# Splitting heads 1 and 2's normed tokens where they lie, and moving two products of head 2 ahead of its projections

## The chip, the cores and the metric

The kernel runs on one core of one Trainium2 chip. The metric is the device time of one launch, in microseconds (us); a lower time is better. The engines are named as in the profile: PE is TensorE (matmuls), PEld its weight loads, DVE is VectorE, ACT is ScalarE, POOL is GpSimd and SP is SyncE, which here only issues DMAs.

## The reference, cut to what matters

Two layers of an encoder step run on 576 tokens (512 of a prompt, 64 of a sample), 1024 features wide. In each layer the tokens are normed and go through one wide projection, whose columns feed a short convolution, a latent attention with eight heads, and two gates:

```python
h = rmsnorm(x, g_pre_mix)
z = h @ w_in
b_g, c_g, xin, cq, ckv_raw, kpe_raw, ga, gb = jnp.split(z, ...)
yc, new_buf = short_conv(c_g * xin, conv_buf, conv_w)
y_a = b_g * yc
q = (rmsnorm(cq, g_q) @ w_uq).reshape(B, L, N_HEADS, QK_DIM)
y_b = mla_attention(q_nope, q_pe, pos, ckv_all, kpe_all, k_pos, w_uk, w_uv)
merged = jax.nn.sigmoid(ga) * y_a + jax.nn.sigmoid(gb) * y_b
x = x + rmsnorm(merged @ w_o, g_post_mix)
x = x + rmsnorm(jnp.square(jax.nn.relu(rmsnorm(x, g_pre_ffn) @ w1)) @ w2, g_post_ffn)
```

## The kernel before, in words

**Precision.** Every fp32 product is made of three matmuls. Each operand is split into a high part (an ACT copy into a rounded format) and a low part (a DVE subtraction, original minus high part), and `mm3` (L809 to L813) adds low weight times high token, high weight times low token and high times high. So each weight block and each token tile passes through one ACT instruction and then one DVE instruction before PE can use it.

**Layout.** Features lie on the 128 partitions, in eight rows of tiles (k = 0 to 7); the 576 tokens lie along the free axis, in two halves of 288. The high and low parts of the tokens are `xs_hi` and `xs_lo` (`pl.xh`, `pl.xl`). A projection of 128 columns for one half is 24 matmuls of 288 columns ("a block half").

**Plain and mixed heads.** Per layer eight heads run one after the other. Heads 0, 1 and 7 are plain: five weight blocks, each for two halves, on tokens that are only scaled by the gain, with the norm factor applied afterwards. Heads 2 to 6 are mixed: two pairs of blocks (c = 0 and 1) are each computed by seven products of half size (12 matmuls each) instead of eight, in Winograd's manner, and two more half-blocks (`mixed_block`) make the fifth. These products need the truly normed tokens, and four tiles of differences of them, called turned: `turn_raw` is made by `head_mix(t)` on DVE, and split into `turn_hi` (ACT) and `turn_lo` (DVE, `head_mix_lo`). Products 0, 1 and 6 use normed tokens, products 2, 3, 4 and 5 use turned tiles 1, 2, 3 and 0 (`TURN_ORDER`).

**Where the normed tokens lie before.** During heads 0 and 1 DVE norms the tokens in place, in `x` (`normed_rows`, semaphore `h_made`). The four `turn_hi` tiles occupy just the memory of `x`, so before they are written SP stores the normed tokens to DRAM (`h_store`, three DMAs of 864, 864 and 576 KB, L961 to L963, at positions 0, 1 and 2 of head 1). When head 1's last block (block 4) has read the old `xs_hi`, SP loads them back into the memory of `xs_lo` (`h_load`, four DMAs of 576 KB, L956 to L959, in the order `H_ORDER`). ACT copies each quarter into `xs_hi` (`normed_hi`, L1590 to L1594) and DVE subtracts in place (`normed_head_lo`, L2484 to L2488).

**Order.** There is no planner: each engine's order is written out by hand, and semaphores join them. PE's order in head 1 is block 0, projections, block 1, scores, block 2, turns (transposes of the probabilities), block 3, attended (probabilities times values), block 4. In a mixed head it is products 0 to 3, projections, products 4 to 6, scores, `mixed_block`, turns, products 0 to 2 of the second pair, attended, products 3 to 6. Head 2 alone begins with its projections, before products 0 to 6. The projections of an even head are: rotary query for two halves (9 matmuls each), keys (6 matmuls of 512), values in two parts (12 matmuls of 256 each), query for two halves (9 each). They wait within for DVE: keys for `pv_read` (DVE has read the old attention result, in `attention_out`), values part 1 and the first query half for the two rotary sums, the second query half for `keys_lo`.

**Ring.** The products go through four PSUM banks in turn. A product may start when the bank that was filled four products earlier has been emptied: product 0 by the ACT copy `snapshot`, product 1 by `upper_left`, 2 by `first_difference`, 3 by `second_sum` and so on, on DVE.

**Other queues.** SP issues all weight loads, the loads of the small attention weights of the next head (`even_small`, five DMAs, L865 to L873) in position 2 of head 1, and the store of each finished head's row. POOL issues, in layer 0 only, DMAs that add up weight blocks for both layers' mixed heads (`weight_sums`); they share the DMA engines with SP's loads. In head 1 ACT splits the small weights (L1228) before it copies the transposed probabilities (L1494), so attended hangs on the small weights' arrival.

Of the kernel before, what the change touches and what calls it, by code (L numbers as in the profile page):

```python
# [15 lines left out]
P = 128  # L16
# [162 lines left out]
H_ORDER = ((0, 0), (4, 0), (4, 1), (0, 1))  # L179
# [176 lines left out]
class Plan:  # L356


    def __init__(self, nc, ctx):
# [4 lines left out]
        self.h_kept = nc.dram_tensor("h_kept", (P, KC, NT), F32, kind="Internal").ap()  # L364
# [138 lines left out]
        self.h_stored = semaphore("h_stored")  # L503
        self.h_landed = [semaphore("h_landed0"), semaphore("h_landed1"), semaphore("h_landed2"), semaphore("h_landed3")]
# [294 lines left out]
def cols(s):  # L799
    return slice(NH * s, NH * (s + 1))  # L800
# [52 lines left out]
def loads(nc, block, pl, x_in, consts, tables, blocks, small, uv, cache_t, cache_n, cache_pe, x_out):  # L853
# [3 lines left out]
    def _(sp):  # L857
# [39 lines left out]
        for L in range(DEPTH):  # L897
# [58 lines left out]
            def h_load(n):  # L956
                k0, half = H_ORDER[n]
                sp.dma_start(pl.xlraw[:, k0:k0 + 4, cols(half)], pl.h_kept[:, k0:k0 + 4, cols(half)]) \
                    .then_inc(pl.h_landed[n], 16)  # L959

            def h_store(n):  # L961
                rows = slice(3 * n, min(3 * n + 3, KC))
                sp.dma_start(pl.h_kept[:, rows, :], pl.x[:, rows, :]).then_inc(pl.h_stored, 16)  # L963

# [18 lines left out]
            for h in range(HEADS):  # L983
# [3 lines left out]
                if h == 1:  # L987
                    sp.wait_ge(pl.h_made, KC * (L + 1))
                if h == HEADS - 1:
                    sp.wait_ge(pl.my_stored, stored(L, HEADS - 2))  # L990
                for j in range(HEAD_POS[h + 1] - HEAD_POS[h]):
# [8 lines left out]
                    if (h, j) == (FIRST_MIXED - 1, 4):  # L1000
                        sp.wait_ge(pl.ring_full, full(L, r_hd(h, 4, 0)))
                        sp.wait_ge(pl.h_stored, 48 * (L + 1))
                        h_load(0)
                        h_load(1)
                        sp.wait_ge(pl.ring_full, full(L, r_hd(h, 4, 1)))
                        h_load(2)
                        h_load(3)
                    elif is_mixed(h):
# [6 lines left out]
                    if h == FIRST_MIXED - 1 and j < 3:  # L1015
                        h_store(j)
# [185 lines left out]
def scalar_engine(nc, block, pl, x_in, x_out, kv_out, kpe_out, conv_out):  # L1202
# [4 lines left out]
    def _(eng):  # L1207
# [121 lines left out]
        for L in range(DEPTH):  # L1329
# [172 lines left out]
            def plain_head(h):  # L1502
# [2479 lines left out]
```

## Time and profile before

| | us |
|---|---|
| median of 3 runs | 1723.73 (1723.25 to 1723.8) |
| the profiled execution, its own time | 1726.3 |
| its span (first to last instruction) | 1724.5 |
| PE busy | 1705.7 (99%) |
| DVE busy | 1309.3 (76%) |
| ACT busy | 855.1 (50%) |

The granted clock of TensorE was 0.997 of full speed over the span. The profile splits the span into slices and names, for each idle time of an engine, what ended it; "L811" is a line of the program, which for matmuls is a line of the helper `mm3`. In the timelines a row gives the start, the duration, the engine, the line, the operation with output and inputs, and a count of merged instructions; square brackets hold the idle time before it and what ended that. Matmuls overlap, so that the step from one start to the next (0.13 us for 288 columns) is what one costs. Head 1's attended part to head 2's turns lies at 134 to 177 us in layer 0 and at 989 to 1028 us in layer 1.

### The profile page before, as it was taken

The page shows a single profiled execution, that of the slowest core. Times are in us where ns is not written, and L with a number is a line of the kernel's source. Part 1 is how long each engine was busy: PE and PEld are TensorE (multiplying, and loading weights), DVE is VectorE, ACT ScalarE, POOL GpSimd, SP SyncE. Part 2 cuts the span into 40 slices and gives each one's busy share as a digit, 9 for nine tenths or more (in the row PEclk, how much of TensorE's full clock was granted, in tenths as well). Part 3 has the DMA queues.
Part 4 walks back from the last instruction along what each step waited for, and adds up shares of the span by engine and source line. Part 5 has one row for each costly group of instructions (what it writes and reads, how often), then busy time and mean ns, then how long its engine had stood idle before and what let it go on. Part 6 is the DMA issues. An engine that isn't in the chain of part 4 may idle for free.

```text
span 1724.5 us, 31894 instructions
## 1 busy us (share of the span) xinstructions
PE 1705.7 (99%) x12735; PEld 1690.9 (98%) x12735; DVE 1309.3 (76%) x2514; ACT 855.1 (50%) x1665; POOL 122.3 (7%) x163
## 2 busy tenths in 40 slices
PE   9999999999999999999999999999999999999997
PEld 9998999999999999999999999999999999999997
DVE  7788787767798786668687797777678887777665
ACT  7625454545465454436366364545435536444452
POOL 1412121212210000000001000000000000000000
PEclk9999999999999999999999999999999999999998
DMA  7899898898762232323124454343532213322231
GB/s 239 198 212 244 214 209 211 178 249 235 163 129 97 89 96 86 99 86 111 60 84 149 148 166 139 114 121 112 171 117 98 99 37 111 98 86 87 74 99 55
DMA packets 90996, 231.54 MB, mean 134 GB/s; under 512 B 9824, under 2 KB 25440, under 8 KB 90848
## 3 DMA queue, kind: packets, MB, share of 16 engines
q1 hardware_dynamic: 71968, 185.45, 33.5%
q0 software_dynamic: 17600, 41.95, 13.8%
q8 instruction: 101, 1.65, 0.4%
q10 hardware_dynamic: 1280, 2.10, 0.3%
q14 instruction: 47, 0.39, 0.1%
HBM read 214.39 MB, written 57.02 MB: 157 GB/s over the span
## 4 chain that ended last, share of the span: by engine, by line
PE 94%; DMA 2%; DVE 2%; ACT 1%; SPq 1%; issue 0%; DVEq 0%; ACTq 0%
PE ring L811 19%; PE ring L813 19%; PE ring L812 19%; PE att L811 11%; PE att L813 11%; PE att L812 11%; PE att L3527 1%; DMA cache_pe_raw<-cache_pe_in 1%; PE att L806 1%; PE att L805 1%; DMA small_raw<-small_in 1%; DMA xs_lo_raw<-h_kept 1%; PE att L818 0%; ACT rope_s L1291 0%; PE att L3343 0%
## 5 line engine op out<-in xcount | busy, mean ns | idle before, releaser
L811 PE MATMUL ring<-xs_hi,w_lo 128*128 128x288 f32 x1872 | 556.6, 297 | 4.3 <-DVE xs_lo L2744 2.2
L813 PE MATMUL ring<-xs_hi,w_hi 128*128 128x288 f32 x1872 | 551.4, 295 | 0.0
L812 PE MATMUL ring<-xs_lo,w_hi 128*128 128x288 f32 x1872 | 551.3, 294 | 0.0
L2071 DVE TENSOR_TENSOR w_lo<-w_raw,w_hi 128x1024 fp32r<-128x1024 f32 (+1 forms) x364 | 370.0, 1035 | 37.3 <-ACT w_hi L1220 27.2
L811 PEld LDWEIGHTS ring<-xs_hi,w_lo 128*128 128x128 f32 x1872 | 351.6, 188 | 7.3 <-DVE ga L2355 2.4
L812 PEld LDWEIGHTS ring<-xs_lo,w_hi 128*128 128x128 f32 x1872 | 351.7, 188 | 1.4
L813 PEld LDWEIGHTS ring<-xs_hi,w_hi 128*128 128x128 f32 x1872 | 351.5, 188 | 0.0
L813 PE MATMUL att<-f_hi,w_hi 128*128 128x288 f32 x960 | 283.2, 295 | 0.0
L812 PE MATMUL att<-f_lo,w_hi 128*128 128x288 f32 x960 | 282.9, 295 | 0.0
L811 PE MATMUL att<-f_hi,w_lo 128*128 128x288 f32 x960 | 282.6, 294 | 0.0
L811 PEld LDWEIGHTS att<-f_hi,w_lo 128*128 128x128 f32 x960 | 180.4, 188 | 0.0
L812 PEld LDWEIGHTS att<-f_lo,w_hi 128*128 128x128 f32 x960 | 180.4, 188 | 0.0
L813 PEld LDWEIGHTS att<-f_hi,w_hi 128*128 128x128 f32 x960 | 180.4, 188 | 0.0
L1212 ACT ACTIVATE w_hi<-w_raw 128x1024 fp32r<-128x1024 f32 x98 | 101.9, 1053 | 87.0 <-DMA w_raw<-blocks_in 86.8
L1220 ACT ACTIVATE w_hi<-w_raw 128x1024 fp32r<-128x1024 f32 x118 | 122.8, 1051 | 7.2 <-DMA w_raw<-blocks_in 6.5
L2923 DVE TENSOR_TENSOR my<-att,my 128x288 f32<-128x288 f32 x160 | 70.8, 451 | 67.7 <-PE att L813 67.7
L813 PE MATMUL ring<-mix_hi,w_hi 128*128 128x288 f32 x384 | 113.5, 295 | 0.0
L811 PE MATMUL ring<-mix_hi,w_lo 128*128 128x288 f32 x384 | 113.1, 295 | 0.0
L812 PE MATMUL ring<-mix_lo,w_hi 128*128 128x288 f32 x360 | 105.9, 294 | 0.0
L811 PE MATMUL ring<-turn_hi,w_lo 128*128 128x288 f32 x320 | 94.9, 296 | 0.0
L812 PE MATMUL ring<-turn_lo,w_hi 128*128 128x288 f32 x320 | 94.4, 295 | 0.0
L813 PE MATMUL ring<-turn_hi,w_hi 128*128 128x288 f32 x320 | 94.2, 295 | 0.0
(342 smaller groups left out, 3184.4 us busy)
## 6 DMA issues: line engine op xcount, KB each, us to landing
w_raw<-blocks_in SPq DMA_DIRECT2D x195, 512.0 KB, 3.7
weight_sums<-blocks_in POOLq DMA_DIRECT2D x80, 256.0 KB, 7.2
w_raw<-blocks_in SPq DMA_DIRECT2D x62, 256.0 KB, 4.6
weight_sums<-blocks_in POOLq DMA_DIRECT2D x20, 512.0 KB, 5.6
weight_sums<-weight_sums POOLq DMA_DIRECT2D x40, 256.0 KB, 7.6
w_raw<-weight_sums SPq DMA_DIRECT2D x20, 512.0 KB, 4.6
w_raw<-weight_sums SPq DMA_DIRECT2D x40, 256.0 KB, 4.4
small_raw<-small_in SPq DMA_DIRECT2D x16, 320.0 KB, 4.6
```

The lines of the kernel that those rows point to most:

```text
L805: pe.matmul(out, both, keys[1], start=False, stop=False)
L806: return pe.matmul(out, both, keys[0], start=False, stop=True)
L811: pe.matmul(out, w[1], x[0], start=first, stop=False)
L812: pe.matmul(out, w[0], x[1], start=False, stop=False)
L813: return pe.matmul(out, w[0], x[0], start=False, stop=last)
L1212: act.activation(hi, raw, ACT.Copy).then_inc(pl.weights_hi, 1)
L1220: act.activation(hi, raw, ACT.Copy).then_inc(pl.weights_hi, 1)
L2071: return dve.tensor_tensor(out, a, hi.bitcast(F32), ALU.subtract)
L2923: dve.tensor_tensor(dst, src, dst, ALU.add).then_inc(pl.w2_free, 1)
L3527: last = pe.transpose(att[:, to:to + P], pl.probs[:, PO[t] + P * j:PO[t] + P * (j + 1)], ident)
```

## The change: what it does

The store and the reload are gone, with their semaphores and SP's wait for `h_made` at the start of head 1. ACT splits the normed tokens straight from `x` into `xs_hi` as soon as block 4 of head 1 has read the old half, and DVE subtracts from `x`; the quarters come in a new order (rows 0 to 3 and 4 to 7 of half 0, then of half 1). The turned high parts, which overwrite `x`, now wait for the low parts of the normed tokens and come after them. PE runs products 0 and 1 of head 2 before the head's projections, the rest after. The split of weight position 12 (`at + 2`), which head 1 did last, moves into head 2.

```diff
-H_ORDER = ((0, 0), (4, 0), (4, 1), (0, 1))
+H_ORDER = ((0, 0), (4, 0), (0, 1), (4, 1))
 # SP
-                if h == 1:
-                    sp.wait_ge(pl.h_made, KC * (L + 1))
-                    if (h, j) == (FIRST_MIXED - 1, 4):
-                        sp.wait_ge(pl.ring_full, full(L, r_hd(h, 4, 0)))
-                        sp.wait_ge(pl.h_stored, 48 * (L + 1))
-                        h_load(0)
-                        h_load(1)
-                        sp.wait_ge(pl.ring_full, full(L, r_hd(h, 4, 1)))
-                        h_load(2)
-                        h_load(3)
-                    if h == FIRST_MIXED - 1 and j < 3:
-                        h_store(j)
 # ACT, end of head 1
-                next_weight(3)
-                if h == FIRST_MIXED - 1:
-                    eng.wait_ge(pl.turn_made, 4 * (L + 1))
-                    eng.wait_ge(pl.h_stored, 48 * (L + 1))
-                    for t in TURN_ORDER:
-                        act.activation(pl.th[t][:, :, :], pl.traw[t][:, :, :], ACT.Copy).then_inc(pl.turn_hi, 1)
-                else:
+                if h != FIRST_MIXED - 1:
+                    next_weight(3)
                     next_weight(4)
 # ACT, head 2
                 def normed_hi(n):
-                    eng.wait_ge(pl.h_landed[n], 16 * (L + 1))
-                    act.activation(pl.xh[tile], pl.xlraw[tile], ACT.Copy).then_inc(pl.h_hi, 1)
+                    eng.wait_ge(pl.ring_full, full(L, r_hd(h - 1, 4, half)))
+                    eng.wait_ge(pl.h_made, KC * (L + 1))
+                    act.activation(pl.xh[tile], pl.x[tile], ACT.Copy).then_inc(pl.h_hi, 1)
+                def turned_hi_of(i):
+                    t = TURN_ORDER[i]
+                    eng.wait_ge(pl.turn_made, 4 * (L + 1))
+                    eng.wait_ge(pl.h_lo, 4 * L + (3 if t < 2 else 4))
+                    act.activation(pl.th[t][:, :, :], pl.traw[t][:, :, :], ACT.Copy).then_inc(pl.turn_hi, 1)
                 def even_projections():
...
                     if h == FIRST_MIXED:
-                        normed_hi(0)
+                        turned_hi_of(1)
                     keys_hi(h)
                     rotary_hi(h)
-                    if h == FIRST_MIXED:
-                        normed_hi(1)
                     values_hi(h, 0)
                     values_hi(h, 1)
                     if h == FIRST_MIXED:
-                        normed_hi(2)
+                        turned_hi_of(2)
+                        turned_hi_of(3)
+                        pos_hi(L, at + 2)
                     query_hi(h)
                     rotary_sample(h)
                 if h == FIRST_MIXED:
+                    for n in range(4):
+                        normed_hi(n)
+                    turned_hi_of(0)
+                    snapshot(0)
                     even_projections()
                     pos_hi(L, at + 3)
-                    normed_hi(3)
-                    snapshot(0)
 # DVE, end of head 1
-                next_weight(3)
+                if h != FIRST_MIXED - 1:
+                    next_weight(3)
-                elif h == FIRST_MIXED - 1:
-                    head_mix_lo(0)
-                    head_mix_lo(1)
                 attention_out(h)
+                    normed_head_lo(0)
                     gated_out(h, 0)
+                        normed_head_lo(1)
                     gated_out(h, 1)
+                        normed_head_lo(2)
                     merge(h, slice(0, NP_), pl.merged)
 # DVE, head 2
                     rotary_sum(h, 0)
                     rotary_sum(h, 1)
-                        normed_head_lo(0)
                     keys_lo(h)
+                        head_mix_lo(0)
                     rotary_lo(h)
-                        normed_head_lo(1)
                     values_lo(h, 0)
                     values_lo(h, 1)
-                        head_mix_lo(2)
+                        head_mix_lo(1)
                     query_lo(h, 0)
                     query_lo(h, 1)
                 if h == FIRST_MIXED:
+                    upper_left(0, pl.cv[:, cols(0)])
+                    normed_head_lo(3)
                     even_projections()
+                    pos_lo(L, at + 2)
+                    head_mix_lo(2)
                     head_mix_lo(3)
-                    upper_left(0, pl.cv[:, cols(0)])
-                    pos_lo(L, at + 3)
                     first_difference(0)
-                    normed_head_lo(2)
+                    pos_lo(L, at + 3)
                     second_sum(0)
-                    normed_head_lo(3)
 # PE, mixed head
-                if h == FIRST_MIXED:
-                    projections(h)
-                for i in range(4):
+                ahead = 2 if h == FIRST_MIXED else 4
+                for i in range(ahead):
                     product(h, 0, i)
-                if h != FIRST_MIXED:
-                    projections(h)
-                for i in range(4, 7):
+                projections(h)
+                for i in range(ahead, 7):
                     product(h, 0, i)
```

PE's own waits for `h_lo` follow the new order: one quarter for product 0, two for product 1, four for product 6.

## Rows read from the trace of the kernel before

**Rows 1.** The page's first part: busy time, share of the span, instructions.
```profile
PE 1705.7 (99%) x12735; PEld 1690.9 (98%) x12735; DVE 1309.3 (76%) x2514; ACT 855.1 (50%) x1665; POOL 122.3 (7%) x163
```
**Rows 2.** PE's waits over the span: total us, times, longest.
```profile
PE att L811 <- DVE probs_t_lo L2071: 2.4, 1, 2.4
PE ring L811 <- DVE xs_lo L2744: 2.2, 1, 2.2
...
PE ring L811 <- DVE xs_lo L2071: 0.7, 2, 0.4
```
**Rows 3.** Timeline of PE in layer 0 (start, us, what, idle before).
```profile
133.74 0.29 PE L813 MATMUL ring<-xs_hi,w_hi 128*128 128x288 f32 x1
136.47 0.50 PE L811 MATMUL att<-probs_t_hi,v_lo 128*128 128x512 f32 x1 [2.44 <-DVE probs_t_lo L2071]
...
148.01 0.50 PE L811 MATMUL att<-ckv_hi,small_lo 128*128 128x512 f32 x1 [0.62 <-DVE rx L2454]
...
177.43 1.26 PE L3527 MATMUL att<-consts,probs 128*128 128x128 f32 x10
```
**Rows 4.** Timeline of PE in layer 1, same stretch.
```profile
989.16 0.39 PE L811 MATMUL att<-probs_t_hi,v_lo 128*128 128x512 f32 x1
...
991.01 0.34 PE L811 MATMUL ring<-xs_hi,w_lo 128*128 128x288 f32 x1
...
997.43 0.29 PE L811 MATMUL att<-cqn_hi,small_lo 128*128 128x288 f32 x1
...
1006.78 0.29 PE L811 MATMUL ring<-xs_hi,w_lo 128*128 128x288 f32 x1
...
1018.47 0.22 PE L818 MATMUL att<-q,small_hi 128*128 128x128 f32 x1
...
1028.45 1.25 PE L3527 MATMUL att<-consts,probs 128*128 128x128 f32 x10
```
**Rows 5.** Timeline of ACT in layer 1.
```profile
991.73 4.32 ACT L1576 ACTIVATE turn_hi<-turn_raw 128x1152 fp32r<-128x1152 f32 x4
998.83 3.32 ACT L1291 ACTIVATE rope_s<-att 32x288 f32<-32x288 f32 x8 [2.77 <-PE att L813]
...
1003.86 1.80 ACT L1467 ACTIVATE q_pe<-rope_t 64x288 fp32r<-64x288 f32 x4
...
1009.64 1.08 ACT L1220 ACTIVATE w_hi<-w_raw 128x1024 fp32r<-128x1024 f32 x1
```
**Rows 6.** Timeline of DVE in layer 1.
```profile
994.17 1.22 DVE L2071 TENSOR_TENSOR w_lo<-w_raw,w_hi 128x1024 fp32r<-128x1024 f32 x1
995.31 2.62 DVE L2071 TENSOR_TENSOR turn_lo<-turn_raw,turn_hi 128x1152 fp32r<-128x1152 f32 x2
...
1000.58 0.46 DVE L2386 TENSOR_TENSOR rope_t<-att,cos 128x288 f32<-128x288 f32 x1 [0.43 <-ACT rope_s L1291]
...
1004.75 0.68 DVE L2071 TENSOR_TENSOR k_lo<-att,k_hi 128x512 fp32r<-128x512 f32 x1
1005.46 1.87 DVE L2071 TENSOR_TENSOR q_pe<-rope_t,q_pe 64x288 fp32r<-64x288 f32 x4
...
1008.64 1.28 DVE L2071 TENSOR_TENSOR v_lo<-att,v_hi 128x512 fp32r<-128x512 f32 x2
...
1011.11 0.81 DVE L2071 TENSOR_TENSOR q<-att,q 128x288 fp32r<-128x288 f32 x2
```
**Rows 7.** The chain that ended last, in order of time (start, us, what).
```profile
122.53 10.03 DMA small_raw<-small_in
...
378.11 12.65 DMA cache_pe_raw<-cache_pe_in
```
**Rows 8.** DMA issues from 207 to 222 us (count, KB, us to landing).
```profile
small_raw<-small_in SPq DMA_DIRECT2D x1, 192.0 KB, 6.7
```
**Rows 9.** DMA issues from 290 to 305 us, same columns.
```profile
small_raw<-small_in SPq DMA_DIRECT2D x1, 192.0 KB, 10.6
```
**Rows 10.** Busy us by engine (instructions), granted clock, DMA share, GB/s, 62 to 140.
```profile
62.00:140.00 78.00, 75.10 (x554) 73.66 (x553) 57.74 (x115) 34.00 (x67) 18.32 (x26) 1.00 0.85 203
```

More of the change, by code:

```diff
@@ L954, in pos_load @@
                     sp.dma_start(pl.half_slot(s, k)[2], piece).then_inc(pl.slots[s], 16)
[L956 to L963, printed above, removed]
             def my_load(n):
@@ L999, in _ @@
                         sp.dma_start(pl.naraw[:, :, :], cache_n[L]).then_inc(pl.nat_landed, 16)
[L1000 to L1008 removed]
+                    if is_mixed(h):
                         sp.wait_ge(pl.ring_full, full(L, r_mixed(h, (1, 3, 5, 8, 9, 11, 13, 15)[j])))
@@ L2487, in normed_head_lo @@
                 eng.wait_ge(pl.h_hi, 4 * L + n + 1)
-                minus(pl.xl[tile], pl.xlraw[tile], pl.xh[tile]).then_inc(pl.h_lo, 1)
+                minus(pl.xl[tile], pl.x[tile], pl.xh[tile]).then_inc(pl.h_lo, 1)
             def plain_head(h):
@@ L2580, in plain_head @@
                     own.step(dve.tensor_tensor(pl.ga[:, :], pl.ga[:, :], pl.rx[:, :], ALU.mult))
-                next_weight(3)
+                if h != FIRST_MIXED - 1:
+                    next_weight(3)
                 if h < FIRST_MIXED - 1:
                     next_weight(4)
-                elif h == FIRST_MIXED - 1:
-                    head_mix_lo(0)
-                    head_mix_lo(1)
                 attention_out(h)
                 own.wait()
+                if h == FIRST_MIXED - 1:
+                    normed_head_lo(0)
                 if h < HEADS - 1:
                     gated_out(h, 0)
+                    if h == FIRST_MIXED - 1:
+                        normed_head_lo(1)
                     gated_out(h, 1)
+                    if h == FIRST_MIXED - 1:
+                        normed_head_lo(2)
                     own_ring(h, 4, 1)
@@ L2653, in even_projections @@
                     rotary_sum(h, 1)
+                    keys_lo(h)
                     if h == FIRST_MIXED:
-                        normed_head_lo(0)
-                    keys_lo(h)
+                        head_mix_lo(0)
                     rotary_lo(h)
-                    if h == FIRST_MIXED:
-                        normed_head_lo(1)
                     values_lo(h, 0)
@@ L2669, in mixed_head @@
                 if h == FIRST_MIXED:
+                    upper_left(0, pl.cv[:, cols(0)])
+                    normed_head_lo(3)
                     even_projections()
+                    pos_lo(L, at + 2)
+                    head_mix_lo(2)
                     head_mix_lo(3)
-                    upper_left(0, pl.cv[:, cols(0)])
+                    first_difference(0)
                     pos_lo(L, at + 3)
-                    first_difference(0)
-                    normed_head_lo(2)
                     second_sum(0)
-                    normed_head_lo(3)
                 else:
@@ L3574, in product @@
                     if i in (0, 1, 6):
-                        eng.wait_ge(pl.h_lo, 4 * L + (0, 1, 6).index(i) + 1)
+                        eng.wait_ge(pl.h_lo, 4 * L + (1 if i == 0 else 2 if i == 1 else 4))
                     else:
```

4 lines of the change are left out of this document (removed).

## The prediction

> **What bounds the kernel now.** The first view is the page's busy part: PE is busy 1705.7 of 1724.5 us [rows 1], so a change can only move PE's waits. The second, PE's waits, is short [rows 2]: the ones that this change can touch are 2.4 us for the transposed probabilities and 0.7 us (two waits, one per layer) for the low parts of the normed tokens; 2.2 us lie at the end of layer 0. The third, PE's timeline over head 1's end and head 2, puts numbers to the whole stretch. I measure it from the point at which attended may start to the turns of head 2. In layer 1 attended starts without a wait at 989.16 and the turns at 1028.45: 39.3 us [rows 4]. In layer 0 the block before attended issues its last matmul at 133.74, so attended could start at 133.87; it starts at 136.47, and the turns at 177.43: 43.6 us [rows 3].
>
> **The stretch without any wait.** From rows 4: attended 1.85 (989.16 to 991.01), block 4 6.42 (to 997.43, which is 48 matmuls at 0.133 each). Products of 12 matmuls are 1.59 each, so seven are 11.1. The projections lie between 997.43 and 1006.78: 9.35, of which some 0.25 is waiting for `keys_lo`; 9.1. Scores and `mixed_block` last from 1018.47 to 1028.45: 10.0. Together 38.5. So layer 1 waits 0.8 us in all, layer 0 5.1 us: 2.6 before attended, the rest in four small waits, the first of them before keys [rows 3]. More than 5.9 us is not to be had from this stretch.
>
> **What goes.** The store and the reload move 4.7 MB per layer. Layer 0's 2.6 us comes from the small weights: their last DMA took 10.03 us to land from its issue at 122.53 [rows 7], with two stores of 864 KB issued before it. Attended started 3.9 us after that landing, so a landing before 130.0 would clear it. Without a store in front, the same 192 KB DMA landed in 6.7 us in one later head and in 10.6 us in another [rows 8, 9]; issued at about 122.1 it lands between 128.8 and 132.7. Two ends, then: the wait goes (2.6), or it stays (0). I take the first, as the stores' bytes were ahead of it here, and keep the other as a rival. From 62 to 140 us the DMA engines moved 203 GB/s [rows 10]. On this the Trainium skill (DMA: Bandwidth & Descriptors, section Queues, rings and completion order) says that each DMA engine takes turns between its queue rows, packet by packet. By that rule SP's row had half of 203 GB/s beside POOL's, an estimate, and 864 KB less in front is up to 8.7 us earlier, which clears the wait outright; the 10.6 us of rows 9, with no store ahead, does not fit so simple a picture.
>
> The small waits of both layers (2.5 and 0.8) come from the old order of DVE work and go with it; what matters is what the new order puts there.
>
> **The new order, worked through on layer 1's clock.** Steps: ACT's split of 1152 columns 1.08 from start to start (four end within 4.32), of a weight 0.95; DVE's 1.27 and 1.14; a result is seen by another engine about 0.05 us after the end, by PE 0.13 [rows 5, 6]. DVE reaches the point where `w_lo` started, 994.17, and now goes straight to `attention_out` (0.7, where before 3.7 us of splits came first).
>
> Block 4's first half is full at 994.4. ACT copies quarter 0 until 995.6, DVE subtracts until 997.0; product 0 could start at 997.43: no wait, by 0.3. `gated_out` (0.37), quarter 1 until 998.7; product 1 at 999.02: no wait, by 0.2. `gated_out` of half 1 (0.5), quarter 2 from 999.1 to 1000.4, `merge` to 1001.0. ACT has finished quarters 2 and 3 at 999.9, but the first turned copy waits for quarter 2's low part: 1000.5 to 1001.6, and `snapshot` ends at 1002.0. DVE stands idle 1.1 us for it, then `upper_left` and quarter 3 until 1003.7. PE has begun the projections at 1000.6.
>
> The rotary swaps take ACT 1.66 per half [rows 5]: 1002.0 to 1005.3. The rotary sums (1.2 each: both lie between the start at 1000.58 and 1003.5, one 1.27 split ahead of `k_lo`, with a wait between them) follow at 1003.8 and 1005.4 and end at 1005.1 and 1006.7; PE wants them at 1005.8 and 1007.3. ACT: turned copy, then keys until 1007.0; `keys_lo` [rows 6] until 1007.7, wanted at 1008.5. So the projections run through and product 2 can start at 1009.7. Its low part, the first turned subtraction, ends at 1009.0: in time.
>
> Then DVE has before product 3: four rotary subtractions (1.88), two of the values (1.2), and the second turned subtraction (1.35) [rows 6]: 1008.9 + 1.9 + 1.2 + 1.35 = 1013.4. Product 3 could start at 1011.3; it starts at 1013.5: **a new wait of 2.2**. Product 4 could start at 1015.1, but behind the turned subtraction lie `query_lo` twice (0.75), the moved weight 12 (1.14) and the third turned subtraction (1.35): 1013.3 + 0.75 + 1.14 + 1.35 = 1016.5, so **a second new wait of 1.5**. The fourth ends at 1017.8, product 5 needs it at 1018.3; `first_difference` and weight 13 end by 1019.3, product 6 needs them at 1019.9. Scores start at 1021.5 and the turns at 1031.45, against 1028.45. DVE's later duties (masks, maxima, probabilities) shift with the scores, as their own chain has 1 us more room than before.
>
> The same procedure, run on the old order with the same steps, gives 1028.36 where the trace has 1028.45, so I trust it to a few tenths. The bounds of the two waits: nothing, if DVE were never idle while waiting for ACT (it idles 2.9 us from 994.17 to 1007, and 2.9 earlier leaves 0.8 of the 3.7), and 1.5 us more per layer, if quarters 0 and 1 come late for products 0 and 1, whose margins are 0.3 and 0.2.
>
> **Sum.** Attended to turns becomes 1031.45 - 989.16 = 42.3 us in both layers, since the order is the same and layer 0's DMAs no longer stand in it. Layer 1: 42.3 - 39.3 = +3.0. Layer 0: 42.3 - 43.6 = -1.3. Together +1.7 us on the profiled execution's 1726.3, so 1728.0 (span 1726.2). The median of the runs was 1723.73, 2.6 lower; +1.7 on it is **1725.4**. PE's clock was at its full level (1.00) in a stretch with the 2.44 us wait in it [rows 10], and no new wait is longer, so I charge nothing for it.
>
> **Rivals.**
> *A, the new waits don't come* (the order lets products 3 and 4 through, because DVE and ACT are quicker together than I add up). All 5.9 us go: 1717.8. For it: 5.9 us of waits are really there. Against: DVE was full in this stretch before, and its work now begins with idle time.
> *B, the small weights still land late in layer 0* (the other side). Place: ACT's split before the transposed probabilities. Price: up to 2.6 us, from a landing after 130.0. With it layer 0 is +1.3 and the sum +4.3: 1728.0. For it: rows 9. Against: 1.7 MB less in front of it.
> *C, the wait at the end of layer 0 goes too.* It followed a cache DMA of 12.65 us [rows 7] beside POOL's sums; fewer bytes and another phase may bring it in early: 2.2 less and some 0.3 of restart, +1.7 - 2.5 = -0.8, so 1722.9. The same phase could make it worse by as much, but less likely.
> *D, the removed DMAs were hidden and the order costs nothing either*: no change from 1723.7 within 1 us; layer 0's 2.6 would have to stay and the new waits be half mine.
>
> **How the numbers follow.** Forecast (within 1.3 us of 1725.4) 0.55; A 0.10; B 0.17; C 0.11; D 0.07. The measurement can tell about 0.2%, 3.4 us, from no change, so faster means below 1720.3 and slower above 1727.2. Faster: A and a little of C, 0.12. Slower: B with the forecast's upper edge, 0.22. Same: 0.66. The range leaves out most of A and the far end of B: 1721 to 1728.8; the forecast's own is 1724.1 to 1726.7.
>
> **What would show it.** PE's waits after: the 2.4 us for the probabilities gone in layer 0 (else B); no wait of products 0 and 1 for quarters 0 and 1; a wait of about 2.2 us before product 3 and 1.5 us before product 4 in both layers, ended by DVE's turned subtraction; from attended to turns 42.3 us twice. If that distance is below 40 us I am wrong in the order of DVE's work (A); if products 0 or 1 wait, in head 1's end; and if both distances are right while the time is not, something outside this stretch moved (C).

## The result, and the profile after

The median after is 1732.43 us (7 runs, 1729.27 to 1734.06) where the kernel before had 1723.8 beside it (7 runs, 1723.25 to 1729.72). The ratio of the two is 1.0033, 95% interval 1.0021 to 1.0045. A second comparison gave 1.0034 (1.0022 to 1.0046), with 1730.76 against 1724.59. So the change costs 5.7 to 5.9 us by the ratio; the forecast was +1.7. The time lies outside the range given, 1721 to 1728.8.

The forecast also stood on a narrow base. The kernel before was run some 150 times more beside the experiments: its medians were 1724.6 to 1726.7 and its single times 1720.9 to 1732.1. The three runs shown ahead of the prediction (1723.25 to 1723.8) lay below all of these medians. Ratios are taken within a comparison and don't suffer from it.

The profiled execution after took 1730.14 us, its span is 1728.3: 3.8 more than before. PE's waits of the kernel after (total, times, longest) come first.

```profile
PE ring L808 <- DVE turn_lo L2051: 7.3, 4, 2.4
PE ring L808 <- DVE xs_lo L2727: 2.7, 1, 2.7
```

Against [rows 2] the 2.4 us for the probabilities and the 0.7 us for the low parts of the normed tokens are gone, and four waits for the turned subtraction have come. PE's timeline of the kernel after shows them, with the points that the forecast measured from:

```profile
133.71 0.39 PE L808 MATMUL att<-probs_t_hi,v_lo 128*128 128x512 f32 x1
...
158.28 0.37 PE L808 MATMUL ring<-turn_hi,w_lo 128*128 128x288 f32 x1 [2.35 <-DVE turn_lo L2051]
...
161.42 0.37 PE L808 MATMUL ring<-turn_hi,w_lo 128*128 128x288 f32 x1 [1.31 <-DVE turn_lo L2051]
...
176.25 1.25 PE L3510 MATMUL att<-consts,probs 128*128 128x128 f32 x10
...
989.99 0.39 PE L808 MATMUL att<-probs_t_hi,v_lo 128*128 128x512 f32 x1
...
1014.57 0.37 PE L808 MATMUL ring<-turn_hi,w_lo 128*128 128x288 f32 x1 [2.35 <-DVE turn_lo L2051]
...
1017.70 0.37 PE L808 MATMUL ring<-turn_hi,w_lo 128*128 128x288 f32 x1 [1.31 <-DVE turn_lo L2051]
...
1032.53 1.25 PE L3510 MATMUL att<-consts,probs 128*128 128x128 f32 x10
```

In layer 0 attended starts at 133.71 without a wait and the turns at 176.25: 42.5 us. In layer 1 they start at 989.99 and 1032.53: again 42.5 us, where the forecast said 42.3 twice. DVE's own timeline of layer 1 has the work that the forecast queued ahead of products 3 and 4:

```profile
1008.58 1.35 DVE L2051 TENSOR_TENSOR turn_lo<-turn_raw,turn_hi 128x1152 fp32r<-128x1152 f32 x1
1009.96 1.87 DVE L2051 TENSOR_TENSOR q_pe<-rope_t,q_pe 64x288 fp32r<-64x288 f32 x4
1011.87 1.29 DVE L2051 TENSOR_TENSOR v_lo<-att,v_hi 128x512 fp32r<-128x512 f32 x2
1013.07 1.35 DVE L2051 TENSOR_TENSOR turn_lo<-turn_raw,turn_hi 128x1152 fp32r<-128x1152 f32 x1
1014.34 0.82 DVE L2051 TENSOR_TENSOR q<-att,q 128x288 fp32r<-128x288 f32 x2
1015.07 1.22 DVE L2051 TENSOR_TENSOR w_lo<-w_raw,w_hi 128x1024 fp32r<-128x1024 f32 x1
1016.20 2.62 DVE L2051 TENSOR_TENSOR turn_lo<-turn_raw,turn_hi 128x1152 fp32r<-128x1152 f32 x2
```

So in this pair of executions layer 0's turns come 1.2 us earlier (forecast 1.3), and layer 1's stretch is 3.25 longer (forecast 3.0). Together 2.05 of the 3.8 us. Another 2.0 came between layer 0's turns and layer 1's attended, where nothing was changed: 811.7 us before and 813.7 after. (Behind layer 1's turns the kernel after is 0.2 quicker.) The row that shows it is the first product with wo in layer 0, and the granted clock behind it. PE's timeline after, and then the windows (columns as in [rows 10]):

```profile
402.16 0.45 PE L808 MATMUL ring<-xs_hi,w_lo 128*128 128x288 f32 x1 [2.73 <-DVE xs_lo L2727]
402.41 0.44 PE L809 MATMUL ring<-xs_lo,w_hi 128*128 128x288 f32 x1
```

```profile
400.00:402.00 2.00, 0.00 (x0) 0.00 (x0) 1.97 (x7) 0.92 (x3) 0.00 (x0) 1.00 0.73 154
402.00:404.00 2.00, 1.84 (x8) 1.87 (x9) 2.00 (x7) 0.12 (x1) 0.54 (x1) 0.58 0.97 302
404.00:406.00 2.00, 2.00 (x11) 2.00 (x10) 2.00 (x5) 0.10 (x1) 1.12 (x2) 0.57 0.55 79
406.00:408.00 2.00, 2.00 (x18) 2.00 (x16) 1.48 (x3) 2.00 (x6) 0.00 (x0) 1.00 0.88 124
```

The wait is 0.5 us longer than the 2.2 of [rows 2]. After PE's wait of 2.73 us the clock goes from its full level (2.4 GHz) towards the lower one (1.2 GHz): matmuls follow each other in 0.24 in place of 0.13 us for 14 steps, some 1.5 us. What ended the wait is further back, in the chain and on ACT. First the chain after, then ACT's timeline:

```profile
376.24 13.75 DMA cache_pe_raw<-cache_pe_in
```

```profile
390.02 1.06 ACT L1532 ACTIVATE cache_t_hi<-cache_t_raw 128x1024 fp32r<-128x1024 f32 x1 [3.32 <-DMA cache_pe_raw<-cache_pe_in]
```

The fetch was issued 1.9 us earlier than before but took 13.75 us in place of 12.65 [rows 7]. Part of what PE had gained by then was given back.

A caution on sizes: the second profiled execution of the kernel after has 3.7 us of wait at this place, and a single pair can't give the median's difference. That needs the experiments.

### The profile page after: what moved, and what is told of

Read it like the earlier page. It is cut to its first block, busy times and chain, and to the rows that moved or that the text cites. A ratio compares the mean times of both kernels' runs of the same rounds, so it can differ in the third digit from the quotient of the medians.

```text
span 1728.3 us, 31890 instructions
## 1 busy us (share of the span) xinstructions
PE 1706.8 (99%) x12735; PEld 1692.9 (98%) x12735; DVE 1311.5 (76%) x2514; ACT 854.5 (49%) x1665; POOL 122.4 (7%) x163
## 4 chain that ended last, share of the span: by engine, by line
PE 95%; DVE 2%; ACT 1%; DMA 1%; issue 0%; SPq 0%; DVEq 0%; ACTq 0%
PE ring L808 19%; PE ring L810 19%; PE ring L809 19%; PE att L808 11%; PE att L810 11%; PE att L809 11%; PE att L3510 1%; DMA cache_pe_raw<-cache_pe_in 1%; PE att L803 1%; PE att L802 1%; ACT rope_s L1267 1%; DVE turn_lo L2051 0%; PE att L815 0%; PE ring L3346 0%; PE att L3326 0%
```

## The experiments

Theories that are called by a letter are stated in the expectations.

**Once more, and three first guesses.** *after_again* is the kernel after, for a second profile. *reorder* puts the weight-12 split back into head 1, takes `snapshot` ahead of the first turned copy, the low parts of the first two quarters ahead of `gated_out`, and all turned splits and `first_difference` ahead of the rotary, value and query splits, on ACT and DVE:

```diff
@@ DVE, head 2
-                    even_projections()
-                    pos_lo(L, at + 2)
+                    head_mix_lo(0)
+                    rotary_sum(h, 0)
+                    rotary_sum(h, 1)
+                    keys_lo(h)
+                    head_mix_lo(1)
                     head_mix_lo(2)
                     head_mix_lo(3)
                     first_difference(0)
                     pos_lo(L, at + 3)
+                    rotary_lo(h)
...
```

> The changed kernel, unchanged, to see what differs from run to run. Its profiled execution took 1730.1 us, of which +3.3 lie in layer 1's head 2, -1.3 in layer 0's heads 1 and 2, +0.5 in a longer wait at the end of layer 0 and +1.6 in a stretch of 3.4 us at 402 us where the granted clock was 0.58; yet most other runs took 1732 to 1734 at a lower mean clock. Theory K (clock): a run's time follows its mean granted clock, about 1.7 us more for each 0.001 below 0.997, because TensorE falls to its lower level after one or more of the waits (2.4 and 1.3 in each layer's head 2, 2.7 at the end of layer 0); the new trace has 402 us or the heads' waits followed by matmuls at 0.24 us a step. Theory D (DMA): the runs differ in the wait at the end of layer 0, which hangs on a cache load; the trace then shows that wait outside 2.2 to 2.8 us with the clock unchanged. Median 1732 by both.

> The changed kernel with DVE and ACT in another order in head 2: the split of weight position 12 back in head 1, the second normed quarter's subtraction ahead of the first gated output, and all turned splits ahead of the rotary, value and query splits. By the same step arithmetic that gave the waits of 2.2 and 1.5 us, none is left: turns 38.7 us after attended in both layers (changed kernel: 42.5). Both theories: both waits gone in both layers, 3.7 us each. Theory K: the falls of the clock after them go too, leaving the one after the end of layer 0 in some runs: median 1721 to 1724.5, 8 to 11 below the changed kernel. Theory D: 7.5 below, 1725.

*after_again*: 1.0034; its waits of PE are 7.2 us (4) for `turn_lo` and 3.7 before wo. The clock was lower in 160 to 170 (0.66) and in 400 to 420 us. *reorder*: 1722.24, ratio 0.9981 (0.9968 to 0.9994). No wait before products 3 and 4 is left in either layer, and layer 1's stretch is 38.7 us. So the new waits were a matter of the order of the splits on DVE and ACT, as forecast, and with another order the change can pay (a gain of 0.2%, near what can be told).

*fill_all* puts matmuls that nobody reads into the waits, to see whether the clock then stays up and what that is worth; *fill_heads* does it in head 2 alone. *before_store_late* moves the second of the three stores of normed tokens in the kernel before behind the small weights, where the third already stood.

```diff
+                    if h == FIRST_MIXED and i in (3, 4):
+                        fill(r_mixed(h, i), 17 if i == 3 else 10)
...
+            if L == 0:    # this part in fill_all only
+                fill(WO_A[0], 40, False)
```

> The changed kernel with idle matmuls put where PE waits: 17 of 288 columns before product 3 and 10 before product 4 of head 2 (both layers), 40 of 128 columns before the first output product of layer 0. They write the bank that the next product overwrites and take no longer than the waits. Theory K: the waits are as long as before but PE is active in them, so the clock stays at its upper level: mean clock 0.997 or more in every run and 1727 to 1728.5 us, 4 to 5 us below the changed kernel and with a spread under 1 us. Theory D: the time stays at 1730 to 1734.

> The kernel after with matmuls into an unused place of PSUM in head 2's new waits: 17 of 288 columns before product 3 (about 2.4 us) and 10 before product 4 (about 1.5 us), in both layers; their results are read by nobody. Nothing is changed at the end of layer 0. Theory K: the waits are filled, no clock fall at 160 or 1017 us, and the waits themselves stay; against the kernel after 1 to 2 us less on the median (ratio to before 1.0025). Theory D: no change against the kernel after (ratio 1.0034), and the wait at 402 to 407 us is there with 2 to 4 us.

> The kernel before with one step moved: SP issues the second store of normed tokens (864 KB) behind the small weights of head 2 instead of in front of them. If the stores in front made these land late (step 2 of the prediction), the wait of 2.4 us before attended in layer 0 shrinks to under 0.5 us and the rest stays: profile 1723.7, median 1721.5 against 1723.8. If POOL's sums alone make them late, the wait stays within 0.5 us of 2.4 and the time within 0.7 us.

*fill_all*: 1.0034 (1.0021 to 1.0047) with the clock at full level in every 10-us window up to 1700; its fill before wo took 4.66 us and outlasted the wait by some 0.8, which hides part of what it gave. *fill_heads*: 1.0033 (1.0018 to 1.0048), waits in the heads filled, 4.0 us of wait before wo with a lower clock behind it. Theory K had asked 4 to 5 us of *fill_all*, so the clock is not the main cause. A smaller part of it, the 1 to 2 us that K gave *fill_heads* (ratio 1.0025), lies inside that run's interval and is not excluded. *before_store_late*: 1.0000 (0.9989 to 1.0011). The wait for the probabilities went in its profile, as expected of a store in front of the small weights (though the same wait, with the stores in place, was 0.2 to 2.4 us in the five profiles of the kernel before and its other variants); 3.6 us for `k_lo` came in its place, because the tokens' reload then stood late in front of `keys_hi` in ACT's order.

**The cache's fetches issued earlier**, in both kernels, and together with the reordering (*best*).

```diff
-                    if h == HEADS - 1 and j == 2:
+                    if h == HEADS - 1 and j == 1:
+                        sp.wait_ge(pl.ring_full, full(L, r_hd(h, 1, 0)))
                         sp.dma_start(pl.ctraw[:, :, 0:PAST], cache_t[L]).then_inc(pl.cache_landed, 16)
```

> The kernel after with one edit: the loads of cache_t and cache_pe at the end of a layer are issued half a block of head 7 earlier. So far the two profiled executions of the kernel after had 2.7 and 3.7 us of wait before the first product of the next tokens' output, at 402 and 407 us, where the kernel before had 2.2. Theory D (the missing 2 to 4 us beyond the forecast lie in this wait, which is ended by the landing of the cache DMA): the wait falls below 0.7 us, and the clock does not fall at 402; the time goes down by 2.7 to 4.5 us against the kernel after, so about 1726 to 1728 where the kernel before has 1724 (ratio 1.001 to 1.002). Theory K (the missing part is TensorE's granted clock, which falls after waits anywhere, 1.6 us each): only the fall at 402 goes, and another can come at 160: 1 to 2 us less than the kernel after, ratio 1.0025. Theory N (the two small waits before products 3 and 4 are larger in median than in the profiled executions): no change, ratio 1.0034.

> The kernel before with the same edit of the cache loads. Its wait at 402 was 2.2 us in its profiled execution, and its clock did not fall there. Theory D: the wait goes, -2 to -2.5 us, ratio 0.9986 to 0.999, so that after_cache_early over before_cache_early still is +1.0 to +2 us (the two head stretches alone: +3.3 and -1.2 in the profiled execution). Theory K: the same or a little less here, since nothing of the clock is to be had back. Theory N: the gap between the two cache_early kernels stays as wide as between after and before, 6 us.

> The reordered version (weight 12 back in head 1, snapshot and first_difference earlier, the four key subtractions ahead of the rotary ones) with the earlier cache loads as well. The reordered version alone had a ratio of 0.9981 with a wait of 1.1 us at 402. Theory D: another 1 us less, ratio 0.9975. Theory K: no window with a lower clock but the one at 140 to 150 us (wait of product 0 or 1 for its low part), ratio 0.9975 as well; neither expects it above 0.9985.

All three missed: 1.0040 (1.0025 to 1.0056), 1.0010 (0.9995 to 1.0025) and 0.9995 (0.9980 to 1.0010). The wait before wo was still 2.8 us in *after_cache_early* and *best*. It was gone in the profile of *before_cache_early*, yet the median was no lower (that profiled execution, 1722.83, was the fastest of its twelve). ACT's timeline of *after_cache_early* says why:

```profile
387.78 1.06 ACT L1206 ACTIVATE small_hi<-small_raw 128x1024 fp32r<-128x1024 f32 x1 [4.84 <-DMA small_raw<-small_in]
```

Another fetch of the same moment, the small weights, was now the late one. ACT takes both splits in its fixed order, so bringing one forward only changed which of the two it waits for. So it is not one fetch that is late; it looks like what the DMA engines get through in these microseconds. What else do they have then? POOL's timeline has the answer. POOL makes sums of weights in DRAM by a chain of DMAs that waits only for itself: each group starts with three copies (the first row of a group is the one shown) and goes on with four adding ones. First before, then after:

```profile
137.12 0.75 POOL L1129 DMA_DIRECT2D weight_sums<-blocks_in  x1 [5.96 <-DMA weight_sums<-weight_sums]
...
395.23 0.76 POOL L1129 DMA_DIRECT2D weight_sums<-blocks_in  x1 [6.55 <-DMA weight_sums<-weight_sums]
```

```profile
130.25 0.75 POOL L1105 DMA_DIRECT2D weight_sums<-blocks_in  x1 [5.75 <-DMA weight_sums<-weight_sums]
...
368.18 0.76 POOL L1105 DMA_DIRECT2D weight_sums<-blocks_in  x1 [5.42 <-DMA weight_sums<-weight_sums]
378.12 0.83 POOL L1112 DMA_DIRECT2D weight_sums<-blocks_in  x1 [7.23 <-issue]
378.66 1.14 POOL L1115 DMA_DIRECT2D weight_sums<-weight_sums  x1
```

The rows at 137.12 and 130.25 are the seventh group of each kernel, those at 395.23 and 368.18 the seventeenth. From 100 to 140 us the DMA engines moved 229 GB/s before and 178 after. In this pair POOL's chain was 7 us ahead at the seventh group and 27 at the seventeenth with the stores and reloads gone. The pair is an extreme one: on the mean of all profiles without a working hold, the seventeenth group starts at 368.8 us in the kernels with the order of the kernel after (seven) and at 383.8 in those with the store (five), 15 us apart, and at the seventh group the lead is 4 us. The small weights and the cache are fetched at 374 to 377 us, right behind the group at 368.

All profiles but *fill_all*, whose wait is filled (group at 368.5). The first column is the start of the one group that begins between 362 and 390 us, the second that less the start of layer 0's turns, the last the time from those turns to layer 1's attended. *before_again* and *before_hold* have one more group just outside, at 360.0 and 360.3.

| profile | group in 362 to 390 | less turns | wait before wo | middle |
|---|---|---|---|---|
| before | 367.0 | 189.6 | 2.2 | 811.7 |
| before_early_group | 363.1 | 187.5 | 0.5 | 809.9 |
| after | 368.2 | 191.9 | 2.7 | 813.7 |
| after_again | 373.7 | 193.6 | 3.7 | 814.7 |
| after_cache_early | 364.1 | 187.5 | 2.8 | 813.9 |
| after_hold | 369.5 | 191.2 | 0.9 | 810.4 |
| after_hold_late | 366.4 | 186.1 | 2.9 | 814.6 |
| fill_heads | 371.3 | 195.1 | 4.0 | 815.6 |
| best | 368.3 | 191.5 | 2.8 | 815.1 |
| reorder_hold | 369.4 | 194.7 | 3.7 | 815.5 |
| reorder | 376.7 | 199.5 | 1.1 | 810.6 |
| before_store_late | 377.2 | 199.2 | none | 809.2 |
| before_cache_early | 377.4 | 200.3 | none | 809.2 |
| before_again | 383.1 | 204.4 | 1.5 | 811.0 |
| before_hold | 386.0 | 209.2 | 0.5 | 810.2 |
| after_held | 380.4 | 204.3 | none | 809.2 |
| reorder_held | 378.7 | 204.5 | 1.5 | 811.1 |
| w12_back_held | 384.0 | 204.6 | 1.5 | 811.1 |
| proj_first_held | 382.2 | 204.4 | 1.3 | 810.8 |

Of ten with a group 186 to 196 us behind the turns, eight waited 2.2 to 4.0 us; of nine with it from 199 on, none waited over 1.5. The border was drawn after these profiles, so this is a pattern to be tested, not a test. Among the kernels with the change and no working hold, all of the order of the kernel after have it at 364 to 374; of those with the store, four of five have the seventeenth group at 377 to 386, and the profiled one at 395, which put its sixteenth on 367. At the end of layer 1 no profile has this wait, and there POOL issues no DMA (its last starts at 484 to 505 us).

**Is it POOL's group that does it?** A wait was put into POOL's chain, on a product of head 7. The sums behind it are read in layer 1 alone. The first attempt counted the groups wrongly, by one, in all four kernels (`n == 16`, in the kernel before `n == 15`):

```diff
             for n in range(n0, n1):
+                if n == 16:
+                    pool.wait_ge(pl.ring_full, full(0, r_hd(HEADS - 1, 2, 0)))
```

> The kernel after with one wait added on POOL: its 17th group of sums (DMAs from the weights, and DMAs that add), which in the profiled executions began at 364 to 374 us, waits until head 7's third product of half 0 is full, about 378 us. The sums made after that are read in layer 1 alone. Theory P (the wait before the first wo product at the end of layer 0 is set by where POOL's own chain of groups stands when the small weights and the cache are fetched: groups begun at 364 to 374 us had 2.2 to 4.0 us of wait in seven profiles, groups begun near 377 us had 0 to 1.1 us in three): the wait falls to 0 to 1.1 us, the clock does not fall at 402, and the median goes down by 3 to 4 us against the kernel after, ratio 1.0012 to 1.002. Theory Q (the wait goes with the bytes that SP asks for, whatever POOL does): the wait stays 2 to 4 us, ratio 1.0034.

> The same with POOL held until head 7's fourth product of half 1 is full, about 388 us, so that POOL has no DMA beside the fetches of the small weights and of the cache once its 16th group is through. Theory P: these fetches land in under 10 us, ACT waits under 1 us for small_raw and cache_pe_raw together, wait before wo under 1 us unless the weights after them come late, ratio 1.0012 to 1.002. Theory Q: waits as before, ratio 1.0034.

> The kernel before with POOL's 16th group, begun at 367 us in its profiled execution (wait before wo 2.2), held to about 378 us. Theory P: no wait before wo, 1 to 2.5 us less than the kernel before, ratio 0.9985 to 0.9995, and after_hold minus before_hold is the two head stretches alone, +2 to +3.5 us. Theory Q: ratio 1.0, after_hold minus before_hold +6.

> The reordered version (ratio 0.9981 and with early cache loads 0.9995, where its POOL group began at 368 us) with the 17th group held to about 378 us. Theory P: wait before wo 0 to 1.1 us, ratio 0.997 to 0.998. Theory Q: 0.998 to 0.9995.

1.0026 (1.0015 to 1.0037), 1.0030 (1.0018 to 1.0041), 0.9995 (0.9982 to 1.0008) and 0.9980 (0.9967 to 0.9992). In the three with the change the group at 366 to 370 us was not held; the wait stood at the one behind it, and only *after_hold_late* was stopped there, by some 4 us, until 395. In *before_hold* it stood at the seventeenth, which came at 386 by itself. These say nothing on the theory; they stand in the table as further profiles. One of them, *after_hold*, is an exception to the pattern (0.9 us). The first two are near to repeats of the kernel after, and their ratios, 1.0026 and 1.0030, are lower than its 1.0033 and 1.0034.

With `n == 15` in the kernel after and the reordered one, and with `n == 14` until head 7's first product of half 1 in the kernel before:

> The kernel after, with the POOL group that began at 364 to 374 us in its profiles (the DMAs that add follow at 376 to 384) held until head 7's third product of half 0 is full, about 378 us, so that its adding DMAs begin at about 389. In 14 profiles so far adding DMAs begun 196 to 205 us behind layer 0's turns went with 0.9 to 4.0 us of wait before the first wo product (10 profiles, mean 2.9), and those outside of it with 0 to 1.1 us (4 profiles). Theory P (they cause it): wait 0 to 1.1 us, no lower clock at 402, median 3 to 4 us below the kernel after, ratio 1.0010 to 1.0020. Theory Q (the two only go together): wait 1 to 4 us and ratio 1.0026 to 1.0034.

> The reordered version with the same group held to about 378 us. Theory P: wait 0 to 1.1 us, ratio 0.9965 to 0.9980. Theory Q: 0.9980 as without it, wait anywhere from 1 to 4 us.

> The kernel before with its POOL group so held that it begins at about 367 to 368 us in every execution (one group earlier in number, held until head 7's first product of half 1 is full) and its adding DMAs at about 379: the phase in which the changed kernel stood. Theory P: wait before wo 2 to 4 us, often with a lower clock behind it, ratio 1.0005 to 1.0015. Theory Q: ratio 1.0.

> The kernel before itself once more, for its profile and as a zero of the comparison: ratio 1.0 within 0.001. Theory P: if the adding DMAs begin outside 196 to 205 us behind the turns the wait is 0 to 1.1 us, else 2 to 4.

*after_held*: 1728.96, ratio **1.0011** (1.0001 to 1.0022), from 1.0034. PE's list of waits has none before wo. POOL's timeline shows the hold, ACT's what it did:

```profile
364.83 0.81 POOL L1118 DMA_DIRECT2D weight_sums<-weight_sums  x1 [6.62 <-issue]
380.37 0.76 POOL L1105 DMA_DIRECT2D weight_sums<-blocks_in  x1 [14.73 <-PE ring L810]
```

```profile
383.19 1.06 ACT L1206 ACTIVATE small_hi<-small_raw 128x1024 fp32r<-128x1024 f32 x1 [0.88 <-DMA small_raw<-small_in]
```

The DMA view from 370 to 378.5 us (per queue: packets, MB, share of 16 engines; per issue: count, KB, us to landing), after and then *after_held*:

```profile
q0 software_dynamic: 448, 1.31, 59.2%
q1 hardware_dynamic: 358, 1.40, 43.9%
...
small_raw<-small_in SPq DMA_DIRECT2D x1, 512.0 KB, 10.0
...
cache_pe_raw<-cache_pe_in SPq DMA_DIRECT2D x2, 128.0 KB, 13.0
```

```profile
q1 hardware_dynamic: 695, 2.73, 91.9%
...
small_raw<-small_in SPq DMA_DIRECT2D x1, 512.0 KB, 9.0
...
cache_pe_raw<-cache_pe_in SPq DMA_DIRECT2D x2, 128.0 KB, 7.8
```

Here q0 is POOL's queue and q1 SP's. With POOL's group beside it, SP's queue moved 1.40 MB in these 8.5 us, without it 2.73; the cache's fetch took 13.0 us with it and 7.8 without. The Trainium skill (DMA: Bandwidth & Descriptors, Queues, rings and completion order) says that a DMA engine takes turns between its queue rows, packet by packet. The trace agrees: SP's queue got 358 packets through beside POOL's 448, and 695 without them.

*reorder_held*: 1722.87, ratio **0.9971** (0.9960 to 0.9981), the lowest ratio of all. That is 1.7 us below *reorder* (0.9981), and the two intervals overlap. Its wait before wo is 1.5 us, above the 1.1 expected. *before_again*: 0.9999 (0.9985 to 1.0012), group at 383, wait 1.5.

*before_early_group* missed, and usefully. It was to put the kernel before into the bad place. Its group came at 363, the adding DMAs at 375 and 382, and there was 0.5 us of wait; the ratio is 0.9985 (0.9975 to 0.9995), and its 12 runs lie within 2.7 us (1722.1 to 1724.8) where those of the kernel before beside it spread over 10. A likely reason, argued and not shown: the hold gave POOL's row 11.5 us of idle time, so no backlog stood before SP's fetches. So the place of one group is not the whole law. Nor is its gain all from the hold: its profile has 0.2 us of wait before attended in layer 0 where the other four of that kernel's order have 1.8 to 2.4, long before POOL is held. What is shown is that holding POOL back at the end of layer 0 takes this wait from the kernel after: the stretch from turns to attended is 809.1 us with it, against 813.7 and 814.7. By the ratios it gives 4.0 us (0.0023) to the kernel after, with both intervals counted anything from 1 to 7, and about 2.6 (0.0015) to the one before. The runs' scatter fell from 8.9 to 3.3 us, but *w12_back_held*, which has the same hold, scatters over 9.5.

**Which part of the change brings the waits in head 2.** Both with the hold of *after_held*:

```diff
@@ w12_back_held
-                if h != FIRST_MIXED - 1:
-                    next_weight(3)
-                    next_weight(4)
+                next_weight(3)
+                if h != FIRST_MIXED - 1:
+                    next_weight(4)
...
@@ proj_first_held
-                ahead = 2 if h == FIRST_MIXED else 4
+                ahead = 0 if h == FIRST_MIXED else 4
```

> after_held with the split of weight 12 back in head 1, as in the kernel before. The step-by-step order puts layer 1's attended-to-turns distance at 41.6 us (42.5 in the kernel after, 39.3 before): 2.3 us before product 3 stay and the 1.5 before product 4 become 0.3. Theory S (the wait before product 4 is DVE work that came late): 41.6 in both layers, 1.9 us less than after_held in all, ratio 1.0000 to 1.0005. Theory T (it is the turned subtraction's own chain): 42.5, ratio 1.0011.

> after_held with all of head 2's products behind its projections again, and snapshot and upper_left behind the projections' work; the new splits from the tokens in place stay. The step-by-step order puts layer 1's distance at 42.1 us, with a wait of 2.1 us for the rotary sum before the values and 1.0 before product 4. Theory S (the splits of the tokens in head 1's end cost DVE and ACT work that no order of the products hides): 42.1, ratio 1.0005 to 1.0011. Theory U (the two products in front are what costs): 39.3 to 40, ratio 0.998 to 1.0.

*w12_back_held*: layer 1's stretch is 41.7 us (expected 41.6), with 2.44 before product 3 and 0.16 before product 4, so theory S (the wait before product 4 is DVE work that came late) holds there. The time did not follow: 1.0014 (1.0000 to 1.0028). In layer 0 its profile has a longer wait of product 0 that takes the gain. Attended began 0.6 us late and the split of weight 12 stands again ahead of the low parts:

```profile
145.06 0.38 PE L808 MATMUL ring<-xs_hi,w_lo 128*128 128x288 f32 x1 [1.81 <-DVE xs_lo L2052]
```

*proj_first_held*: 42.3 in layer 1 (expected 42.1), with 2.0 us for the rotary sum in place of the wait before product 3, and 3.1 in layer 0; ratio 1.0005 (0.9993 to 1.0016). That is what its theory S said: neither of the two orders of the products tried hides the splits. The order of DVE's and ACT's own work did (*reorder*, 38.7).

## Why the prediction was wrong

- **The new waits** (2.2 and 1.5 forecast): 2.35 and 1.31 measured, in both layers, ended by the turned subtraction. Right, and so was rival A's refusal.
- **Attended to turns** (42.3 twice): 42.5 twice. Right. Margins of products 0 and 1: in *after* none waits; in *after_again* one does, 0.7 us. They were as thin as the forecast had them: product 0 also waits 0.7 us in *after_hold* and *after_hold_late*.
- **Layer 0's small weights** (2.6 us go): they went in the kernel after, and 0.6 us came back in *after_again*. Right; rival B did not come. But the wait that goes was taken from one execution: it is 1.8 to 2.4 us in four profiles of the kernel before's order and 0.2 in the fifth.
- **The sum of the stretch, +1.7**: +2.05 in the profiled pair. With POOL held, the changed kernel stands at 1.0011, +1.9 us, against the kernel before without a hold. That it meets the forecast so closely is in part luck: against *before_early_group*, with POOL held in both, it is +4.5 (1.0011 and 0.9985), and its own layer 1 lost 2.3 us to the clock.
- **The end of layer 0**, which the sum left at nothing, is the step that failed first. From layer 0's turns to layer 1's attended the kernel after took 2.0 us more in the profiled pair. On the mean of five profiles of its order it is 813.4, against 810.5 in four of the kernel before's: +2.9. Rival C named the place (a cache DMA beside POOL's sums, "fewer bytes and another phase") and then gave it the wrong sign: "The same phase could make it worse by as much, but less likely." The hold took about 4.0 us from here by the ratios (1.0034 to 1.0011), more than the 1.7 us of everything that was worked out. The failure was one of method: the change took 4.7 MB from the queue of layer 0, and the forecast asked what those bytes had delayed in the stretch (the small weights) but not who else would run faster, and into what. POOL's chain waits for nothing but its own DMAs; its period is 22 to 29 us, and the rows of its groups from 137 to 395 us were in the trace of the kernel before.
- **"I charge nothing for the clock"**: wrong as a rule. In six profiles with the kernel after's order in head 2, six of twelve stretches show a lower clock there, behind waits like the 2.44 that had none in [rows 10]; *after_held* lost 2.3 us so in layer 1. The kernel before pays too: three of its four profiles with a wait of about 2 us before attended have it from 130 to 150 us. By the profiles that does not cancel: on the same means, layer 0's turns start 0.8 us later after than before, where the forecast had 1.3 earlier, and the two latest of the five (180.1 and 180.4) are the two with the long falls. So this is the second term put at nothing, some 2 us by five profiles against four, together with the waits of product 0 and of attended. The runs don't confirm the size, as filling the waits gained nothing (1.0034 and 1.0033); how the miss divides between the two terms stays open.
- **The base**: 1723.73 was 1 to 3 us below the later medians of this kernel.

Open: why *after_hold* escaped with 0.9 us (POOL's queue moved 1.29 MB from 370 to 378.5 us there, much as in the kernel after, but the small weights landed in 7.7 us in place of 10.0), why *before_early_group* did, and how the 4 us divide between the wait and the slower steps behind it; one profile per kernel can't tell.

## What to carry to other kernels

When a change takes bytes away from a shared DMA path, list every chain that paces itself on that path, move each forward by what it gains, and see what it meets; an engine 7% busy can set the end of a layer. If such a chain has slack, tie it to a point of the main engine's work: one wait gave back some 4.0 of the 5.8 us that the changed kernel had lost. A term put at nothing, a wait outside the stretch or a lower clock behind a new wait, needs a reason as much as the others do. And when two fetches are awaited in a fixed order, bringing one forward only shows the other.

## What was not expected of the hardware

The granted clock is not given back or taken in the same way each time behind the same wait. In *after* PE waited 2.35 and 1.31 us at 158 and 161 us with no loss; in *after_again* 2.44 and 1.12 us at the same place were followed by this (windows, columns as before):

```profile
158.00:160.00 2.00, 0.19 (x1) 0.22 (x2) 2.00 (x4) 2.00 (x7) 0.33 (x1) 1.00 1.02 231
160.00:162.00 2.00, 1.82 (x12) 1.48 (x11) 2.00 (x4) 1.03 (x2) 0.00 (x0) 0.82 0.97 234
162.00:164.00 2.00, 1.06 (x4) 1.09 (x5) 2.00 (x3) 0.00 (x0) 0.13 (x1) 0.50 0.95 207
164.00:166.00 2.00, 2.00 (x11) 2.00 (x10) 2.00 (x6) 0.00 (x0) 1.55 (x2) 0.50 0.63 144
166.00:168.00 2.00, 2.00 (x10) 2.00 (x10) 0.93 (x3) 0.00 (x0) 0.00 (x0) 0.50 0.95 89
```

That is the lower level for over 5 us. Layer 0's stretch was 46.0 us there against 42.5, of which 0.7 is another wait. Not every fall costs that. Of the six in the six profiles with the kernel after's order in head 2, three cost 2.3 to 2.8 us and three only about 0.2: there the slow matmuls ran on into the second wait, which is gone from the list. So a wait's price here is its own length, or up to some 3 us more, and a forecast should carry both.
